# Memory attention: a head's division before the former head's copy, four samples on four column groups, a fourth load buffer

## The reference, cut to what matters

```python
def mem_attention(q, mem_kv):
    b, L = q.shape[:2]
    qh = q.reshape(b, L, MEM_HEADS, MEM_HD)
    s = jnp.einsum('blhd,bmhd->bhlm', qh, mem_kv[:, :, 0]).astype(jnp.float32) * (MEM_HD ** -0.5)
    p = jax.nn.softmax(s, axis=-1)
    o = jnp.einsum('bhlm,bmhd->blhd', p, mem_kv[:, :, 1].astype(jnp.float32))
    return o.reshape(b, L, MEM_Q).astype(q.dtype)
```

## Time and profile before

| | us |
|---|---|
| median of 3 runs | 3422.87 (3421.79 to 3426.29) |
| the profiled execution, its time | 3424.1 |
| its span | 3422.4 |
| PE busy | 3194.8 (93%) |
| DVE / ACT / POOL busy | 1475.7 / 1150.5 / 273.1 |
| mean granted TensorE clock | 0.965 |

### The profile page before, as it was taken

One profiled execution on the slowest core, in us unless ns is written; L12 is line 12 of the kernel. 1 busy time (PEld: TensorE's weight loads), 2 busy tenths in 40 slices (PEclk: granted clock), 3 DMA queues, 4 the chain that ended last, 5 costly groups with the idle time before them and its releaser, 6 DMA issues.

```text
span 3422.4 us, 55224 instructions
## 1 busy us (share of the span) xinstructions
PE 3194.8 (93%) x22296; PEld 2932.4 (86%) x22296; DVE 1475.7 (43%) x2112; ACT 1150.5 (34%) x1631; POOL 273.1 (8%) x364
## 2 busy tenths in 40 slices
PE   6999998999999979989999899999897889899996
PEld 5899997888887856989999789999895567899996
DVE  4444426776767232254442534442431052544423
ACT  3433323444444223233332323332212142333322
POOL 0000000222222010000000000000001101000000
PEclk9999999999999989999999999999998898999998
DMA  6422322322232224222232242232322602223231
GB/s 200 132 86 86 89 85 59 100 74 76 84 90 71 94 74 135 86 62 86 86 89 85 59 143 86 86 89 84 103 83 67 216 10 62 63 86 88 84 91 51
DMA packets 444958, 306.48 MB, mean 90 GB/s; under 512 B 12516, under 2 KB 415644, under 8 KB 444700
## 3 DMA queue, kind: packets, MB, share of 16 engines
q1 hardware_dynamic: 421780, 231.03, 23.2%
q0 software_dynamic: 19744, 69.48, 6.0%
q10 hardware_dynamic: 3328, 4.47, 0.4%
HBM read 282.73 MB, written 22.20 MB: 89 GB/s over the span
## 4 chain that ended last, share of the span: by engine, by line
PE 89%; DVE 6%; ACT 2%; issue 1%; DMA 1%; ACTq 0%; POOL 0%; SPq 0%; DVEq 0%; POOLq 0%
PE PS L967 58%; PE PS L1210 8%; PE PS L1036 5%; PE PS L1013 2%; PE PS L1158 2%; PE PS L1170 1%; PE PS L1131 1%; PE PS L1109 1%; DVE yT L1516 1%; DVE rb L1501 1%; PE PS L1268 1%; PE PS L1247 1%; PE PS L1341 1%; PE PS L1148 1%; PE PS L1280 1%
## 5 line engine op out<-in xcount | busy, mean ns | idle before, releaser
L1497 DVE TENSOR_TENSOR wlo<-raw,whi 128x1024 fp32r<-128x1024 f32 (+2 forms) x401 | 488.7, 1219 | 786.5 <-ACT whi L545 776.5
L967 PE MATMUL PS<-hH,whi 128*128 128x272 f32 x3280 | 682.7, 289 | 15.5 <-DVE hL L1512 7.6
L967 PE MATMUL PS<-hH,wlo 128*128 128x272 f32 x3280 | 681.1, 289 | 0.0
L967 PE MATMUL PS<-hL,whi 128*128 128x272 f32 x3280 | 678.5, 288 | 0.0
L545 ACT ACTIVATE whi<-raw 128x1024 fp32r<-128x1024 f32 (+2 forms) x401 | 412.9, 1030 | 618.6 <-PE PS L967 553.6
L967 PEld LDWEIGHTS PS<-hH,whi 128*128 128x128 f32 x3280 | 518.9, 189 | 18.3 <-issue 16.7
L967 PEld LDWEIGHTS PS<-hL,whi 128*128 128x128 f32 x3280 | 517.9, 189 | 0.0
L967 PEld LDWEIGHTS PS<-hH,wlo 128*128 128x128 f32 x3280 | 514.2, 190 | 0.0
L967 PE MATMUL PS<-H,whi 128*128 128x272 f32 x1984 | 411.4, 289 | 5.7 <-DVE L L1938 2.5
L967 PE MATMUL PS<-H,wlo 128*128 128x272 f32 x1984 | 411.9, 289 | 0.0
L967 PE MATMUL PS<-L,whi 128*128 128x272 f32 x1984 | 410.3, 288 | 0.0
(11 more groups left out here) (362 smaller groups left out, 3763.4 us busy)
## 6 DMA issues: line engine op xcount, KB each, us to landing
raw<-in_w_ffn_gu SPq DMA_DIRECT2D x176, 512.0 KB, 3.7
kvr<-in_cache_mem_kv POOLq DMA_DIRECT2D x32, 1024.0 KB, 5.9
raw<-in_w_in_a SPq DMA_DIRECT2D x57, 512.0 KB, 3.7
raw<-in_w_ffn_down SPq DMA_DIRECT2D x64, 448.0 KB, 3.6
rawm<-in_w_mem_kv SPq DMA_DIRECT2D x32, 512.0 KB, 4.5
raw<-in_w_ffn_down SPq DMA_DIRECT2D x32, 512.0 KB, 4.0
raw<-in_w_out_a SPq DMA_DIRECT2D x24, 512.0 KB, 3.7
raw<-in_w_in_b SPq DMA_DIRECT2D x20, 512.0 KB, 3.6
```

What stands on the lines that cost most here:

```text
L967: mm = pe.matmul(PS[:, bank + h, 0:HT], w[:, slot, k * P:(k + 1) * P], x[:, h * HT:(h + 1) * HT], start=first and w is whi and x is hi_k, ...
L1497: dve.tensor_tensor(wlo[:, slot, 0:nk * P], src, whi[:, slot, 0:nk * P].bitcast(F32), ALU.subtract).then_inc(s["w_lo"], 1)
```

## The change

- **Heads.** `Pb` has two slots. ACT makes the exponentials of heads 0 and 1 first, and then, after each head's `PT` copy, those two heads ahead. DVE divides head h+1 and takes the maxima of head h+2 before it waits for head h's product and copies it.
- **Samples' keys.** `QZ` is 32 columns wide per batch. Four batches share a group of 16 products, each batch's going to its own 32 partitions of PSUM (`PS[32 * q:32 * q + 32, ...]`). A load brings half the columns of two batches' keys (rows of 2 KB, where they were 4 KB) instead of one batch's whole keys, so that four steps make a group. Six `KT` buffers instead of four; six steps of transposes stand ahead of the first group.
- **Samples' values.** Two batches are taken together, with their products in turn on two of the four groups of 32 partitions. Batches b and b+4 share a group of partitions.
- **Loads.** Four buffers `kvr`; a value load is released by its pair. The sizes in all are the same: 18 loads of 1024 KB a layer.
- `QZ` and `PZ` are a quarter of their size, so POOL's two memsets are, and the arenas are laid out anew. The copies to `PZ`, `QZ` and `M1` follow the new layout.

```diff
-        QZ = Arena([H0, Y0])("QZ", [P, 8, NB, P])
-        PZ = A2("PZ", [P, 2, NB, P])
-        Pb = A2("Pb", [P, NCH, NM])
-        Ob = at("Ob", [P, NCH * NM], M20 + 8192)
-        PT = A2("PT", [P, 2, SEQ])
-        kvr = A2("kvr", [P, 3, 2, D])
-        KT = [A2(f"KT{j}", [P, 4, NM]) for j in range(4)]
+        A2H = Arena([H0, H0 + 8 * tile_b], [H0 + 12 * tile_b, Y0])
+        QZ = A2H("QZ", [P, 8, NB, 32])
+        Pb = A2("Pb", [P, 2, NCH, NM])
+        Ob = at("Ob", [P, NCH * NM], M20)
+        PT = A2H("PT", [P, 2, SEQ])
+        kvr = A2("kvr", [P, 4, 2, D])
+        KT = [A2(f"KT{j}", [P, 4, NM]) for j in range(4)] + [A2H(f"KT{j}", [P, 4, NM]) for j in (4, 5)]
+        PZ = A2("PZ", [P, 2, NB, 32])
...
+                def exps(h):
+                    act.wait_ge(s["mx_ready"], MH * l + h + 1)
+                    if h >= 2:
+                        act.wait_ge(s["ptr_ready"], MH * l + h - 1)
+                    for r in range(NCH):
+                        ins = act.activation(Pb[:, h % 2, r, :], PS[:, 4 + 2 * (h % 2) + r // 2, (r % 2) * NM:(r % 2 + 1) * NM], ACT.Exp, bias=am[:, h % 2, r:r + 1], accum_out=ar[:, h % 2, r:r + 1])
+                    ins.then_inc(s["p_exp"], 1)
+                exps(0)
+                exps(1)
                 for h in range(MH):
-                    act.wait_ge(s["mx_ready"], MH * l + h + 1)
-                    if h:
-                        act.wait_ge(s["ptr_ready"], MH * l + h)
-                    for r in range(NCH):
-                        ins = act.activation(Pb[:, r, :], PS[:, 4 + 2 * (h % 2) + r // 2, (r % 2) * NM:(r % 2 + 1) * NM], ACT.Exp, bias=am[:, h % 2, r:r + 1], accum_out=ar[:, h % 2, r:r + 1])
-                    ins.then_inc(s["p_exp"], 1)
                     act.wait_ge(s["ptr_ready"], MH * l + h + 1)
                     if h:
                         act.wait_ge(s["pv_ready"], MH * l + h)
                     act.activation(PT[:, :, :], PS[:, 0:2, :], ACT.Copy).then_inc(s["pt_evac"], 1)
+                    if h + 2 < MH:
+                        exps(h + 2)
                 for st in range(16):
                     act.wait_ge(s["ks_tr"], 16 * l + st + 1)
-                    if st >= 4:
-                        act.wait_ge(s["ss_ready"], 16 * l + st - 3)
+                    if st >= 6:
+                        act.wait_ge(s["ss_ready"], 4 * l + (st - 6) // 4 + 1)
                     b = (0, 2, 6)[st % 3]
-                    act.activation(KT[st % 4][:, :, :], PS[:, b:b + 2, :].rearrange("p a (j m) -> p (a j) m", j=2), ACT.Copy).then_inc(s["ks_ev"], 1)
...
                 def rows_of(st):
-                    b, half = st // 2, st % 2
-                    idx = 2 + b
-                    if half == 0:
+                    idx = 2 + st // 2
+                    if st % 2 == 0:
                         land(idx)
                     if st >= 3:
                         pe.wait_ge(s["ks_ev"], 16 * l + st - 2)
                     for j in range(4):
                         for t in range(2):
-                            tr = pe.transpose(PS[:, pairs[st % 3] + j // 2, (j % 2) * 256 + t * P:(j % 2) * 256 + (t + 1) * P], kvr[:, idx % 3, t, (4 * half + j) * P:(4 * half + j + 1) * P], ident)
+                            c = t * 512 + j * P
+                            tr = pe.transpose(PS[:, pairs[st % 3] + j // 2, (j % 2) * 256 + t * P:(j % 2) * 256 + (t + 1) * P], kvr[:, idx % 4, st % 2, c:c + P], ident)
                     tr.then_inc(s["ks_tr"], 1)
-                rows_of(0)
-                rows_of(1)
-                for st in range(16):
-                    if st + 2 < 16:
-                        rows_of(st + 2)
-                    pe.wait_ge(s["ks_ev"], 16 * l + st + 1)
+                for st in range(6):
+                    rows_of(st)
+                for i in range(4):
+                    a, half = i // 2, i % 2
+                    pe.wait_ge(s["ks_ev"], 16 * l + 4 * i + 4)
                     for j in range(4):
-                        mm = pe.matmul(PS[:, 4, 0:NM], QZ[:, 4 * (st % 2) + j, st // 2, :], KT[st % 4][:, j, :], start=st == 0 and j == 0, stop=st == 15 and j == 3)
+                        for q in range(4):
+                            mm = pe.matmul(PS[32 * q:32 * q + 32, 4, 0:NM], QZ[:, 4 * half + j, 4 * a + q, :], KT[(4 * i + q) % 6][:, j, :], start=i == 0 and j == 0, stop=i == 3 and j == 3)
                     mm.then_inc(s["ss_ready"], 1)
+                    for st in range(4 * i + 6, min(4 * i + 10, 16)):
+                        rows_of(st)
...
-                for b in range(NB):
-                    land(10 + b)
+                for b0 in range(0, NB, 2):
+                    land(10 + b0)
+                    land(11 + b0)
                     for t in range(2):
                         for k in range(2):
-                            mm = pe.matmul(PS[:, 6 + k, :], PZ[:, t, b, :], kvr[:, (10 + b) % 3, t, k * 512:(k + 1) * 512], start=b == 0 and t == 0, stop=b == NB - 1 and t == 1)
-                    mm.then_inc(s["vb_done"], 1)
+                            for b in (b0, b0 + 1):
+                                q = b % 4 * 32
+                                mm = pe.matmul(PS[q:q + 32, 6 + k, :], PZ[:, t, b, :], kvr[:, (10 + b) % 4, t, k * 512:(k + 1) * 512], start=b < 4 and t == 0, stop=b >= 4 and t == 1)
+                    mm.then_inc(s["vb_done"], 2)
...
+                def divided(h):
+                    dve.wait_ge(s["p_exp"], MH * l + h + 1)
+                    dve.reciprocal(ai[:, h % 2, :], ar[:, h % 2, :]).then_inc(s["p_rcp"], 1)
+                    dve.wait_ge(s["p_rcp"], (MH + 1) * l + h + 1)
+                    dve.tensor_tensor(Pb[:, h % 2], Pb[:, h % 2], ai[:, h % 2, :].unsqueeze(2).to_broadcast([P, NCH, NM]), ALU.mult).then_inc(s["p_ready"], 1)
                 maxima(0)
+                maxima(1)
+                divided(0)
                 for h in range(MH):
                     if h + 1 < MH:
-                        maxima(h + 1)
-                    dve.wait_ge(s["p_exp"], MH * l + h + 1)
-                    dve.reciprocal(ai[:, 0, :], ar[:, h % 2, :]).then_inc(s["p_rcp"], 1)
-                    dve.wait_ge(s["p_rcp"], MH * l + h + 1)
-                    dve.tensor_tensor(Pb[:, :, :], Pb[:, :, :], ai[:, 0, :].unsqueeze(2).to_broadcast([P, NCH, NM]), ALU.mult).then_inc(s["p_ready"], 1)
+                        divided(h + 1)
+                    if h + 2 < MH:
+                        maxima(h + 2)
                     dve.wait_ge(s["pv_ready"], MH * l + h + 1)
                     dve.tensor_copy(M1[:, o0 + 2 * h:o0 + 2 * h + 2, 0:SEQ], PS[:, 2:4, :]).then_inc(s["pv_evac"], 1)
...
-                    if idx >= 3:
-                        what, last = [("kt_tr", l + 1), ("pv_ready", MH * (l + 1))][idx - 3] if idx < 5 else \
-                            ("ks_tr", 16 * l + 2 * (idx - 4)) if idx < 13 else ("vb_done", NB * l + idx - 12)
+                    if idx >= 4:
+                        what, last = ("kt_tr", l + 1) if idx == 4 else ("pv_ready", MH * (l + 1)) if idx == 5 else \
+                            ("ks_tr", 16 * l + 2 * (idx - 5)) if idx < 14 else ("vb_done", NB * l + (idx - 14) // 2 * 2 + 2)
                         pool.wait_ge(s[what], last)
-                    src = mk[l].rearrange("p t (c n) -> p t c n", c=2)[:, :, c, :] if b is None else mkc[l, b][:, :, c, :]
-                    pool.dma_start(kvr[:, idx % 3], src).then_inc(kv_in[idx % 3], 16)
-                    if idx == 2:
+                    dst = kvr[:, idx % 4]
+                    if b is None:
+                        src = mk[l].rearrange("p t (c n) -> p t c n", c=2)[:, :, c, :]
+                    elif c:
+                        src = mkc[l, b][:, :, c, :]
+                    else:
+                        b0, half = b // 4 * 4 + b % 2 * 2, b // 2 % 2
+                        dst = dst.rearrange("p b (t n) -> p b t n", t=2)
+                        src = mkc[l, b0:b0 + 2, :, :, 0, half * 512:(half + 1) * 512].rearrange("b p t n -> p b t n")
+                    pool.dma_start(dst, src).then_inc(kv_in[idx % 4], 16)
+                    if idx == 3:
...
```

More of the change, by code:

```diff
@@ L351, in build_trunk, with by_batch @@
         A2 = Arena([M20, 229344])
-        QZ = Arena([H0, Y0])("QZ", [P, 8, NB, P])
-        PZ = A2("PZ", [P, 2, NB, P])
-        Pb = A2("Pb", [P, NCH, NM])
-        Ob = at("Ob", [P, NCH * NM], M20 + 8192)
-        PT = A2("PT", [P, 2, SEQ])
-        kvr = A2("kvr", [P, 3, 2, D])
-        KT = [A2(f"KT{j}", [P, 4, NM]) for j in range(4)]
+        A2H = Arena([H0, H0 + 8 * tile_b], [H0 + 12 * tile_b, Y0])
[6 more added lines that the diff above has]
+        PZ = A2("PZ", [P, 2, NB, 32])
+        def by_batch(ap, *steps):
+            return bass.AP(ap.tensor, ap.offset, [list(ap.ap[0])] + [list(x) for x in steps])
         am = A2("am", [P, 2, NCH])
@@ L385, in spans @@
             return [(g, f, (i + 1 - f) * P) for g, f in ((0, max(0, i - 1)), (1, 0), (2, 0))]
```

(19 more changed lines are left out.)

24 lines of the change are left out of this document (11 added, 13 removed).

## The result

The changed kernel takes **3335.1 us** (median of four runs, 3325.88 to 3341.1), beside 3422.33 (3421.07 to 3426.29) for the kernel before: a ratio of 0.9741, with a 95% interval of 0.9712 to 0.9769, 87 us less. The forecast was 3354, of a range from 3335 to 3382. The direction held, and so did the mechanism in the heads.

A forecast was written before the change was run, and what follows sets the result against it. Untouched dense products lead 58% of the chain, so only the two attention stretches can shrink: 17.2 + 16.9 + 17.0 + 18.1 = 69.2 us off 3424.1, 3354.9, so 3354 as median. Range 3335 to 3382, its own 3347 to 3362.

The forecast's parts named there:

- What bounds: Whole kernel: 58% of the chain is untouched dense products; the change can act only in the two stretches of memory attention.
- The heads: Memory attention's four heads: DVE's 3.7 us leaves the ring, 28.6 us a layer; 17.2 and 16.9 us off.
- ring: Rival, heads: the ring closes elsewhere, at the copy behind the waiting division; half the gain stays away, 3371; chance 0.05.
- the low clock: Rival, keys: narrow products or waits take the clock to 1.2 GHz; 3386 for half the time; chance 0.08.
- The samples' keys: Keys' products on 32 columns: two run at a time, 3.45 us a group; keys end 31.1 us after last head's product.
- the change between tile widths: Keys: switching between 128 and 32 columns, two changes a group, taken at 0.1 us each, 0.8 us a layer.
- the wait for ACT's last copy: Keys: the last group of products also waits for ACT's last copy, 1.0 us, 1.1 in the sum.
- The rule that was on the other side: Rival "four at a time", from the Trainium skill: four column groups run together, 1.73 us a group, 3340; chance 0.22.
- The loads: Loads in both layers: 2.8 to 3.6 us for 1024 KB, 3.1 taken; 13 still to come after the last head's product.
- The values: Samples' values: pairs take 3.45 us, waits on loads 5.6 and 1.5, end at 58.6; 17.0 us off in layer 0.
- Layer 1's end: After layer 1's values: 12.1 us of transfer stays, 66.0 us after the last head's product; 18.1 us off.
- no overlap: Rival, keys and values: products on different columns don't overlap, only the heads' 34.1 us stay, 3392; chance 0.13.

The follow-up runs named there:

- Old heads: Changed kernel with the order of DVE and ACT in the heads as it was before; 3370.3 us, ratio 0.9842.
- Two products in a row: Changed kernel with each batch issuing two products in a row in the samples' keys, then the next batch; 3343.8 us, one run.
- the same group in a row: Changed kernel with the loops turned round, so each batch's four products follow each other; 3358.6 us, ratio 0.9817.
- two column groups: Changed kernel with the keys' 16 products of a group alternating between two groups of 32 columns; 3349.9 us, ratio 0.9781.
- the nine runs: Four runs of the changed kernel and five of it again, unaltered; between 3325.88 and 3343.21 us.
- three buffers: Changed kernel with three buffers `kvr` instead of four, each load released by the load three before it; 3383.5 us, ratio 0.9884.

## Why the prediction was right, and where it was not

- **What bounds.** Right: all of the change's gain lies in the two attentions, and the dense part moves only with its clock.
- **The heads.** Right to 0.1 us in both layers, 28.5 and 28.6 against 28.6, with the order of the pieces as laid out. The 0.1 has some luck in it: head 0 takes 9.3 us and not 9.6, head 1 7.8 and not 7.9, heads 2 and 3 5.7 each and not 5.55, and these cancel. "Old heads" shows that it is the order that does it. The rival "ring" is out, and so is "the low clock": the clock in the keys is 1.00.
- **The samples' keys: the step that failed.** "If PE starts records in program order, the next product can begin only when the second record does, so two run at a time." A group of 16 takes 1.86, not 3.45. That the second record of a product has to follow the first is so, but it does not hold up what comes behind it, since one product can wait at its own group of columns while others pass. "Two products in a row" and "the same group in a row" show how far this goes. The keys last 23.3 us instead of 29.6, 6.3 less in each layer. What that is worth is read from the kernel with two column groups, which has the forecast's two at a time: its keys last 30.2 us and its samples' stages 124.1, where the forecast's sum has 127.6 and the changed kernel 112.6. So the step is 11.5 us of the 15.1 by which the sum was short. Within it the change between tile widths was near its 0.1, and the wait for ACT's last copy is 2.0 and not 1.1, since two of ACT's copies stand at its end.
- **The rule that was on the other side.** 7.02 to 1.86 is 3.8 times for four groups of columns. The Trainium skill, "TensorE: Matmul & The Clock Gate", Part 3, gives 2.38 times for three, and starts about 4 ns apart. The trace agrees in kind, with four products' first records 7 ns apart. I had given it 0.22 and my own reading 0.48, on an argument that no row bore out. With nothing in the trace for either, the chances should have been turned round or even.
- **The loads.** The bounds of 2.8 to 3.6 us were just missed, at 2.75. Rows of 2 KB are no dearer. By the prediction's own figure, loads at 2.8 instead of 3.1 are worth 3 us.
- **The values.** Right that pairs 0 and 1 run through and that one wait on loads stands before the third pair: forecast 5.6, measured 8.06, since PE gets there sooner. Right too that the fourth pair waits for its load: it lands 5.5 us after the one that the third pair starts with, where the forecast had 6.2, and slow records hide the wait. Pairs 0 and 1 take 5.6 us and not 8.1, for they overlap and have no slow start; pairs 2 and 3 9.15 and not 10.9, which is 5.5 from landing to landing and 3.65 of work. That two pairs could overlap was not in the prediction. The stage, from its start to the last product, is 22.8 against 24.6.
- **Layer 1's end.** Right in kind, the chain runs through `kvn`. 59.1 after the last head's product and not 66.0, because the loads are faster and, with PE ahead, are asked for sooner. From the last value load's landing (2617.4) to that of `kvn` it is 13.1 us, of 12.1 forecast.
- **The range.** 3335 is just the time that came, and taken from the 3422.87 that the forecast starts from, a ratio of 0.9741 is 3334.2, below it; four of the nine runs lie below it too. Its end was the rival's 3340 less 5; loads at 2.75 and 10 us between executions of the same kernel belonged below it as well.

That the overlap and the fourth buffer need each other was not in the prediction at all. It had priced the column groups with four buffers given, and the buffer at nothing of its own; "three buffers" shows that without it, and with loads released by the pair, 46.4 of the 50 us in the samples' stages go. One of its sums is a little off: the end of the values in "no overlap" adds up to 78.5 and not 79.2, which changes no chance.

## What to carry to other kernels

Products that use 32 columns of the array are worth splitting over its four column groups: order them one or two in a row for each group, and they run four at a time (1.86 and 1.90 us here, and 4.52 with four in a row; three were not tried). But price such a gain together with the loads that feed it: here the overlap without the fourth buffer gave 4 us, the buffer without the overlap in the keys 10, and both 50. And where PE waits for loads, look for the landing of the last one before you blame the low clock behind the wait: with the next load on its way the slow records cost nothing (fourth pair here), with the next load issued only at their end they do (three buffers).

## What the runs showed of the hardware

- All the orders tried fit one rule: each group of 32 columns holds one float32 product that runs and one that waits, and others pass them. 16 products take 7.02 us on one group, 3.58 on two, 1.86 on four with one in a row, 1.90 with two and 4.52 with four in a row.
- So a product can start before one that stands ahead of it in the program, on other columns: in the values of layer 0 pair 1's first record starts at 1273.36 us, pair 0's last two products at 1273.99.
- Two loads of 1024 KB that are issued together land their first after 7.1 us, a single one after 5.7; in a row, queued, 1024 KB take 2.75.
- The same kernel has executions 10 us apart with attention stages of the same length: 3329.86 and 3340.03, at mean granted clocks of 0.970 and 0.966.
